# Rotary turns taken off TensorE: latent queries' last columns projected twice, local heads turned by quarters on VectorE, norm factors spread by transposes

## The chip, the cores and the metric

One core of a Trainium2 chip runs the whole program. The metric is the device time of one execution in microseconds, the median over several runs. In the rows PE is TensorE, DVE is VectorE, ACT is ScalarE, POOL is GpSimd and SP the engine whose queue issues the weight loads.

## What is computed

A first block over 512 tokens of width 1024 (spatial gating, sparse attention, cross attention to a memory, feed-forward), then two mixer layers over the 512 tokens and 256 context tokens. In each mixer layer a local branch (heads of 64) and a latent branch (heads of 64 + 32) use rotary turns. The parts that matter here:

```python
def rms_norm_2(x, g):
    xf = x.astype(jnp.float32)
    y = xf * lax.rsqrt(jnp.mean(xf * xf, axis=-1, keepdims=True) + EPS)
    return (y * g.astype(jnp.float32)).astype(x.dtype)

def apply_rope(x, cos, sin):
    xf = x.astype(jnp.float32)
    x1, x2 = jnp.split(xf, 2, axis=-1)
    c = cos[None, :, None, :]
    s = sin[None, :, None, :]
    return jnp.concatenate([x1 * c - x2 * s, x2 * c + x1 * s], axis=-1).astype(x.dtype)

def mla_project(q_lat, kv_lat, g_qa, w_qb, g_kva, w_kvb):
    B, T = q_lat.shape[:2]
    q = (rms_norm_2(q_lat, g_qa) @ w_qb).reshape(B, T, H_B, NOPE_B + ROPE_B)
...
    qa = apply_rope(qa_x.reshape(B, S, H_A, HD_A), cos_a, sin_a)
    ka = apply_rope(ka_x.reshape(B, S, HKV_A, HD_A), cos_a, sin_a)
...
    qr_x = apply_rope(qr_x, cos_b, sin_b)
```

Only the 512 tokens are turned; the context is not. H_A = 8, HKV_A = 2, H_B = 8, NOPE_B = 64, ROPE_B = 32.

## The kernel before, in words

Activations lie with features on the partitions and the tokens along the row: 768 columns (512 tokens, 256 of context), or 512 in the second layer's queries (`nt`). Each weight block arrives by DMA in one of three buffers WB; ACT copies it rounded into WH (`split_hi`), DVE takes the remainder into WL (`split_lo`), and PE multiplies high by high, high by low, low by high, so every linear is three products. `begin(name, part)` on ACT and DVE does the splits that are planned ahead at that point: before `wkvb` of half 0 it splits the query weights `wqb` of half 1; in half 1 the four first units of the next weights (`his(...)` on ACT, `los(...)` on DVE) stand there too.

Every engine's program is written by hand, and order in it is fixed. Four PSUM tiles PS0 to PS3 are given out in turn (`slot(key, *freed)`): PE waits for the marks that the last user of a tile named as `freed`. A mark is a count on a semaphore (`done`, `at`); several marks share one, as `rt`, `rc`, `qr`, `qra` share s_rope, and `qbc`, `kbc`, `qar` share s_up_a.

The latent branch, for each of two halves of four heads: PE projects the four query tiles `qb` (96 rows each, L1547 to L1562), then two key tiles `kb` with two rotations behind each (L1565 to L1580), then two value tiles `vb`, then the attention b. ACT copies a query tile from PSUM to QB (mark `qbc`). A rotation is a product of a constant matrix rotB with QB in plain f32 over 512 columns; DVE (`rope`, L2579) multiplies its result by the sines out of PSUM (`rt`), QB by the cosines (`rc`), and adds (`qr`). In program order DVE does its `begin`s, and in half 1 `los`, before the first rope. The tiles are taken anew from PS0 in each half: `qb` 0 to 3 take PS0 to PS3, `kb` 0 takes PS0, the first rotations PS1 and PS2.

The local branch: linear `kq` makes one key tile, four query tiles and one value tile (L1621); behind the first half of the next tile PE turns the tile before by the matrix rotA (`turn_tile`). ACT brings a tile to SBUF (`qar`, `kar`) before, and splits it after (`q_high`); DVE turns it (`rope_a`) and takes the low part (`q_low`). DVE's fixed order is: turn the keys, their low parts, a weight split, turn tiles 0 and 1, `q_low(0)`, `los` of four units, turn tile 2, `q_low(1)`, turn tile 3, `q_low(2)`, `q_low(3)`, and then attention a, whose softmax maxima DVE takes (L2603) before ACT can do the exponentials.

A norm's factor is one column of RS per 128 tokens; `spread_columns` (L1019) and `spread_between` (L1443) spread it over the partitions by an f32 product of the broadcast column with the identity. Marks `nrec` before and `nbc` behind. `warm` (L838) puts idle products of the identity into PE's waits.

## Time and profile before

| | us |
|---|---|
| median of 3 runs (lowest, highest) | 2468.96 (2465.03, 2470.64) |
| the profiled execution's own time | 2467.05 |
| its span in the trace | 2465.2 |
| PE busy | 2370.0 |
| DVE busy | 1545.7 |
| ACT busy | 1028.4 |
| POOL busy | 533.7 |
| mean granted TensorE clock | 0.989 of full speed |

The engines work side by side, so busy times don't add up. A stage is read from who waits for whom: in the timeline's rows the bracket gives the idle time of the engine before the instruction and what ended it. PE's records are modelled at their ends: two neighbours overlap, and the pace of PE is the distance from start to start.

### The profile page before, as it was taken

The numbers are of one execution on the slowest core, as the hardware profiler recorded it, in microseconds if no ns is written. First come the engines' busy times: TensorE is split into PE (matmuls) and PEld (weight loads), VectorE is DVE, ScalarE is ACT, GpSimd is POOL, SyncE is SP. The second block draws the span as 40 slices with busy tenths as digits, with TensorE's granted clock in tenths as the row PEclk, the third lists the DMA queues.
The fourth block names the chain that finished last, engine by engine and source line by source line (L and its number), as shares of the span: only waits on it lengthen the run. The fifth ranks groups of instructions, "written<-read, shape, count | busy, mean of one in ns | idle before, by whom it ended". The sixth has DMA issues, their size and how long they took to land.

```text
span 2465.2 us, 37427 instructions
## 1 busy us (share of the span) xinstructions
PE 2370.0 (96%) x14791; PEld 1986.9 (81%) x14791; DVE 1545.7 (63%) x2602; ACT 1028.4 (42%) x1955; POOL 533.7 (22%) x380
## 2 busy tenths in 40 slices
PE   8988999999999999999999999999999999999998
PEld 6765767777788887679977899998876688889898
DVE  4757545553434336677467867975656786788774
ACT  3337542532222235563246433334435543654343
POOL 3005212320210212231014211023623200322021
PEclk9998999999999999999999999999999999999999
DMA  5231152354532311002300122223120024013332
GB/s 193 71 104 52 36 188 69 120 160 147 168 107 88 130 50 39 27 1 69 103 26 2 43 78 60 61 78 136 50 58 29 26 69 120 10 44 114 101 110 88
DMA packets 197168, 198.72 MB, mean 81 GB/s; under 512 B 15832, under 2 KB 189624, under 8 KB 196866
## 3 DMA queue, kind: packets, MB, share of 16 engines
q1 hardware_dynamic: 191106, 178.23, 23.4%
q10 hardware_dynamic: 5888, 18.09, 2.0%
q8 instruction: 119, 1.95, 0.3%
q14 instruction: 55, 0.45, 0.1%
HBM read 186.87 MB, written 9.44 MB: 80 GB/s over the span
## 4 chain that ended last, share of the span: by engine, by line
PE 83%; DVE 9%; ACT 4%; issue 3%; POOL 1%; SPq 0%; DMA 0%; ACTq 0%; DVEq 0%; POOLq 0%
PE PS L941 9%; PE PS L942 9%; PE PS L944 9%; PE PS L895 6%; PE PS L897 6%; PE PS L896 6%; PE PS L1063 5%; PE PS L1093 4%; PE PS L868 4%; PE PS L871 4%; PE PS L869 4%; PE PS L1077 3%; DVE WL L2447 1%; PE PS L1135 1%; DVE ST L2603 1%
## 5 line engine op out<-in xcount | busy, mean ns | idle before, releaser
L2447 DVE TENSOR_TENSOR WL<-WB,WH 128x2048 fp32r<-128x2048 f32 (+3 forms) x86 | 185.8, 2160 | 208.6 <-ACT WH L1692 199.2
L941 PE MATMUL PS<-HH,WH 128*128 128x512 f32 (+4 forms) x768 | 298.1, 388 | 4.4 <-DVE XTb L3019 1.5
L942 PE MATMUL PS<-HL,WH 128*128 128x512 f32 (+4 forms) x768 | 284.9, 377 | 0.0
L944 PE MATMUL PS<-HH,WL 128*128 128x512 f32 (+4 forms) x768 | 271.4, 377 | 0.0
L3576 POOL TENSOR_SCALAR SA<-SA,ST 128x768 f32<-128x768 f32 (+4 forms) x80 | 143.7, 1796 | 512.8 <-DVE ST L2615 512.8
L1708 ACT ACTIVATE WH<-WB 128x512 fp32r<-128x512 f32 x240 | 141.9, 624 | 148.5 <-DVE WB L2459 111.8
L1692 ACT ACTIVATE WH<-WB 128x2048 fp32r<-128x2048 f32 (+3 forms) x86 | 148.0, 1721 | 131.9 <-PE PS L944 67.4
L2472 DVE TENSOR_TENSOR WL<-WB,WH 128x512 fp32r<-128x512 f32 x240 | 182.6, 775 | 32.1 <-ACT WH L1708 32.0
L895 PE MATMUL PS<-SH,WH 128*128 128x384 f32 (+1 forms) x576 | 180.6, 314 | 1.2 <-DVE WB L2506 1.2
L941 PEld LDWEIGHTS PS<-HH,WH 128*128 128x128 f32 (+2 forms) x768 | 141.6, 184 | 48.4 <-issue 8.9
L897 PE MATMUL PS<-SH,WL 128*128 128x384 f32 (+1 forms) x576 | 180.0, 313 | 0.0
L896 PE MATMUL PS<-SL,WH 128*128 128x384 f32 (+1 forms) x576 | 179.2, 311 | 0.0
L2603 DVE TENSOR_REDUCE ST<-PS 128x1 f32<-128x768 f32 (+4 forms) x176 | 129.8, 737 | 60.8 <-PE PS L1063 49.5
L942 PEld LDWEIGHTS PS<-HL,WH 128*128 128x128 f32 (+2 forms) x768 | 141.8, 185 | 30.2 <-issue 2.9
L944 PEld LDWEIGHTS PS<-HH,WL 128*128 128x128 f32 (+2 forms) x768 | 135.0, 185 | 23.6
L895 PE MATMUL PS<-HH,WH 128*128 128x384 f32 (+1 forms) x432 | 134.9, 312 | 3.6 <-DVE U L2501 2.9
L896 PE MATMUL PS<-HL,WH 128*128 128x384 f32 (+1 forms) x432 | 134.4, 311 | 0.0
L897 PE MATMUL PS<-HH,WL 128*128 128x384 f32 (+1 forms) x432 | 134.2, 311 | 0.0
L1077 PE MATMUL PS<-CM,SA 128*128 128x128 f32 x736 | 110.2, 276 | 9.0 <-ACT PTa L1805 5.0
L3551 POOL TENSOR_TENSOR RB<-RB,SA 128x512 f32<-128x512 f32 (+2 forms) x59 | 81.6, 1384 | 154.0 <-ACT SA L1758 130.7
L3724 POOL TENSOR_TENSOR YL<-SA,YH 128x768 fp32r<-128x768 f32 (+1 forms) x24 | 43.1, 1800 | 324.8 <-ACT YH L2234 324.8
L1063 PE MATMUL PS<-KB,QB 96*128 96x512 f32 (+1 forms) x288 | 105.2, 487 | 7.2 <-ACT SA L1817 7.0
(461 smaller groups left out, 6056.3 us busy)
## 6 DMA issues: line engine op xcount, KB each, us to landing
WB<-in_w_in_dram SPq DMA_DIRECT2D x61, 1024.0 KB, 5.3
WB<-in_w_ff_dram SPq DMA_DIRECT2D x32, 1024.0 KB, 5.5
WB<-in_w_mod_dram SPq DMA_DIRECT2D x24, 1024.0 KB, 5.3
WB<-in_w_branch_dram SPq DMA_DIRECT2D x24, 512.0 KB, 3.4
WB<-in_w_o_dram SPq DMA_DIRECT2D x8, 1024.0 KB, 5.4
WB<-in_w_in_dram SPq DMA_DIRECT2D x14, 512.0 KB, 6.5
WB<-in_cmp_w_dram SPq DMA_DIRECT2D x4, 1024.0 KB, 5.6
WB<-in_w_mkv_dram SPq DMA_DIRECT2D x4, 1024.0 KB, 5.1
```

The lines of the kernel that those rows point to most:

```text
L895: pe.matmul(D, wh[:, k, :], xh, start=k == 0 and not add, stop=False, skip_group_check=True)
L896: pe.matmul(D, wh[:, k, :], xl, start=False, stop=False, skip_group_check=True)
L897: t = pe.matmul(D, wl[:, k, :], xh, start=False, stop=k == 3, skip_group_check=True)
L941: pe.matmul(D[0:m, d + o:d + o + w], h, xh[:, o:o + w], start=first, stop=False)
L942: pe.matmul(D[0:m, d + o:d + o + w], h, xl[:, o:o + w], start=False, stop=False)
L944: t = pe.matmul(D[0:m, d + o:d + o + w], lo, xh[:, o:o + w], start=False, stop=last)
L1063: t = pe.matmul(S[:, o:o + n], lhs, r, start=i == 0, stop=i == len(rhs) - 1)
L1077: t = pe.transpose(T[0:w, i * 128:(i + 1) * 128], src[:, o:o + w], cm("ident"))
L1692: act.activation(b.of(WH[homes[s][0]]), b.of(WB[b.n % NW]), ACT.Copy).then_inc(*done("wh", s))
L2447: dve.tensor_tensor(b.of(WL[i]), b.of(WB[b.n % NW]), b.of(WH[i]).bitcast(F32), ALU.subtract).then_inc(*done("wl", s))
L2472: dve.tensor_tensor(place(WL, u), src, place(WH, u).bitcast(F32), ALU.subtract).then_inc(*done("wul", n))
L2603: t = dve.tensor_reduce(nm, A.S(s)[:, lo:hi], AX.X, ALU.max, negate=True)
```

## The change

Latent queries: the block `wqb` is marked `turned`. In WH and WL each head now has 128 columns: its 96, then columns 80 to 95 again, then columns 64 to 79 again. The split is three instructions on each of ACT and DVE instead of one. The projection gives 128 rows, the last 32 being the two halves of the rotary part exchanged; the sign is in the table of sines, which now has 64 rows (RPb 64 to 127). DVE multiplies rows 96 to 127 by the sines straight out of the query's PSUM tile (`turned_sines`, mark `rt`), and then the copy in QB by the cosines and adds (`add_cosines`). The sixteen rotation products of the query heads are gone, and the PSUM tile of a query now is freed by `qbc` and `rt`. The latent key's rotation stays on PE.

Local heads: rotA and `turn_tile` are gone (ten rotation products). DVE's `rope_quarters` makes the sine part with four instructions on 32 partitions each, reading one quarter and writing its neighbour, then the cosine product and the sum on 128 partitions.

Norm factors: `spread_columns`, `spread_between` and the spread of GM in front of the last linear use `pe.transpose` instead of `pe.matmul`.

```diff
+    def copies(self, W, B):
+        if not self.turned:
+            return [(self.of(W), self.of(B))]
+        w = W[:, :, :].rearrange("p a b -> p (a b)")[:, 0:self.kt * 512].rearrange("p (a b) -> p a b", b=128)
+        b = self.of(B).rearrange("p k (h c) -> p (k h) c", c=96)
+        return [(w[:, :, 0:96], b), (w[:, :, 96:112], b[:, :, 80:96]), (w[:, :, 112:128], b[:, :, 64:80])]
...
-                    t = pe.matmul(P("norm", N)[:, c * 128:(c + 1) * 128], RS[:, rs[N], c:c + 1].to_broadcast([128, 128]), cm("ident"),
-                                  start=True, stop=True)
+                    t = pe.transpose(P("norm", N)[:, c * 128:(c + 1) * 128], RS[:, rs[N], c:c + 1].to_broadcast([128, 128]), cm("ident"))
...
-                        D = slot(("qb", l, half, i), ("qbc", l, half, i))
+                        D = slot(("qb", l, half, i), ("qbc", l, half, i), ("rt", l, half, i))
...
-                        for i in (2 * p, 2 * p + 1):
-                            D = rope((half, i), ("rt", l, half, i))
-                            pe.wait_ge(*at("qbc", l, half, i))
-                            pe.matmul(D[0:96, 0:512], cm("rotB")[0:96, :], QB[0:96, i, 0:512], start=True, stop=True).then_inc(*done("rot", l, half, i))
...
-                for i, _ in enumerate(linear(f"kq{l}", hx(NT), lambda j: nt if 0 < j < 5 else NT,
-                                             lambda j: [("kar", l) if j == 0 else ("tokc", f"va{l}") if j == 5 else ("qar", l, j - 1)], pace=4)):
-                    if i % 2 and i > 1:
-                        turn_tile(i // 2 - 1)
+                drain(linear(f"kq{l}", hx(NT), lambda j: nt if 0 < j < 5 else NT,
+                             lambda j: [("kar", l) if j == 0 else ("tokc", f"va{l}") if j == 5 else ("qar", l, j - 1)]))
...
+                    def turned_sines(i):
+                        key = (l, half, i)
+                        dve.wait_ge(*at("up", "q", *key))
+                        D = taken(("rope", *key), ("qr", *key))
+                        dve.tensor_tensor(D[64:96, 0:512], P("qb", *key)[96:128, 0:512], RPb[96:128, 1, :], ALU.mult).then_inc(*done("rt", *key))
+
+                    def add_cosines(i):
+                        key = (l, half, i)
+                        x = QB[64:96, i, 0:512]
+                        dve.wait_ge(*at("qbc", *key))
+                        dve.tensor_tensor(x, x, RPb[64:96, 0, :], ALU.mult).then_inc(*done("rc", *key))
+                        dve.wait_ge(*at("rc", *key))
+                        dve.tensor_tensor(x, x, SD[sd["rope", *key]][64:96, 0:512], ALU.add).then_inc(*done("qr", *key))
                     begin(f"wqb{l}", half)
                     begin(f"wkvb{l}", half)
                     if half:
                         los(phases[run[0]][0] + 4)
-                    for p in range(2):
-                        for i in (2 * p, 2 * p + 1):
-                            rope_b((half, i), QB[0:96, i, 0:512], ("qbc", l, half, i), ("qr", l, half, i))
+                    turned_sines(0)
+                    for i in range(4):
+                        if i < 3:
+                            turned_sines(i + 1)
+                        add_cosines(i)
...
+                    for p in range(0, 128, 32):
+                        q = p + 32 if p % 64 == 0 else p - 32
+                        t = dve.tensor_tensor(D[p:p + 32, 0:512], x[q:q + 32, :], RPa[q:q + 32, 1, :], ALU.mult)
+                    t.then_inc(*done("rt", *key))
+                    dve.wait_ge(*at("rt", *key))
+                    dve.tensor_tensor(x, x, RPa[:, 0, :], ALU.mult).then_inc(*done("rc", *key))
+                    dve.wait_ge(*at("rc", *key))
+                    dve.tensor_tensor(x, x, D[:, 0:512], ALU.add).then_inc(*done(*out))
```

Where it changes the order, at three places. PE, layer 0, half 0 of the latent branch, from the last query product to the first key tile, before:

```order
L1559 MATMUL PS<-QLh,WL 96x256
L1572 MATMUL PS<-KVLh,WH 128x512 [waits s_up_v,s_up_a,s_wl]
L1573 MATMUL PS<-KVLl,WH 128x512
L1572 MATMUL PS<-KVLh,WH 128x256
L1573 MATMUL PS<-KVLl,WH 128x256
```

and now:

```order
L1566 MATMUL PS<-QLh,WL 128x256
L1579 MATMUL PS<-KVLh,WH 128x512 [waits s_rope,s_up_v,s_up_a,s_wl]
L1580 MATMUL PS<-KVLl,WH 128x512
L1579 MATMUL PS<-KVLh,WH 128x256
L1580 MATMUL PS<-KVLl,WH 128x256
```

The first product of the key tile, which writes PS0, has got a wait for s_rope; the query products have 128 rows.

DVE, layer 0, half 0: the remainder of `wkvb` (1024 columns), that of the next `wqb`, then the turns. Before:

```order
L2447 TENSOR_TENSOR WL<-WB,WH 128x1024 [waits s_wh,s_up_v]
L2447 TENSOR_TENSOR WL<-WB,WH 128x1152 [waits s_wh]
L2585 TENSOR_TENSOR SD<-PS,RPb 32x512 [waits s_hl_d,s_rpb,s_rot]
L2586 TENSOR_TENSOR QB<-QB,RPb 32x512
L2589 TENSOR_TENSOR QB<-QB,SD 32x512 [waits s_rope]
```

and now:

```order
L2445 TENSOR_TENSOR WL<-WB,WH 128x1024 [waits s_wh,s_up_v]
L2445 TENSOR_TENSOR WL<-WB,WH 128x12x96 [waits s_wh]
L2445 TENSOR_TENSOR WL<-WB,WH 128x12x16 x2
L3261 TENSOR_TENSOR SD<-PS,RPb 32x512 [waits s_hl_d,s_up] x2
L3267 TENSOR_TENSOR QB<-QB,RPb 32x512 [waits s_up_a]
L3269 TENSOR_TENSOR QB<-QB,SD 32x512 [waits s_rope]
```

The first sine product, whose mark PE now waits for, still stands behind the two splits.

DVE, layer 0, local branch: the keys' turn. Before:

```order
L2447 TENSOR_TENSOR WL<-WB,WH 128x2048 [waits s_wh]
L2585 TENSOR_TENSOR SD<-PS,RPa 128x512 [waits s_rpa,s_rope,s_rot,s_up_a]
L2586 TENSOR_TENSOR SA<-SA,RPa 128x512
L2589 TENSOR_TENSOR SA<-SA,SD 128x512 [waits s_rope]
L3397 TENSOR_TENSOR KAl<-SA,KAh 64x768 [waits s_up_a]
```

and now:

```order
L2445 TENSOR_TENSOR WL<-WB,WH 128x2048 [waits s_wh]
L3398 TENSOR_TENSOR SD<-SA,RPa 32x512 [waits s_rope,s_up_a,s_rpa]
L3398 TENSOR_TENSOR SD<-SA,RPa 32x512 x3
L3401 TENSOR_TENSOR SA<-SA,RPa 128x512 [waits s_rope]
L3403 TENSOR_TENSOR SA<-SA,SD 128x512 [waits s_rope]
L3424 TENSOR_TENSOR KAl<-SA,KAh 64x768 [waits s_up_a]
```

Six instructions stand where three stood, and none waits for PE's rotation (s_rot) any more.

## Rows read from the trace of the kernel before

**Rows 1.** The page: shares of the chain of work that ended last.

```profile
PE 83%; DVE 9%; ACT 4%; issue 3%; POOL 1%; SPq 0%; DMA 0%; ACTq 0%; DVEq 0%; POOLq 0%
```

**Rows 2.** Timeline (start us, duration us, engine line op), PE, two rotations, layer 0.

```profile
944.63 1.88 PE L1580 MATMUL PS<-QB,CM 96*96 96x512 f32 x4
945.95 0.80 PE L1572 MATMUL PS<-KVLh,WH 128*128 128x512 f32 x1
```

**Rows 3.** Sources L1580, L1612: duration ns min/median/max, first and last start.

```profile
L1580 PE MATMUL PS<-QB,CM x32: 590/592/594, 944.6 to 1921.8; 96*96 96x512 f32 x32
...
L1612 PE MATMUL PS<-SA,CM x20: 590/590/595, 1234.2 to 2099.7; 128*128 128x512 f32 x20
```

**Rows 4.** The spreads by source, and the timeline of PE at sixteen transposes.

```profile
L1024 PE MATMUL PS<-CM,RS x128: 270/275/579, 40.8 to 1836.7; 128*128 128x128 f32 x128
...
L1448 PE MATMUL PS<-CM,RS x24: 270/275/561, 1763.9 to 1802.1; 128*128 128x128 f32 x24
...
2432.88 1.91 PE L1674 MATMUL PS<-CM,XTc 128*128 128x128 f32 x16
2434.54 0.36 PE L1665 MATMUL PS<-WH,HH 128*128 128x256 f32 x1
```

**Rows 5.** Timeline, layer 0, half 0: first key tile, query weights' split, first sines.

```profile
942.55 0.39 PE L1572 MATMUL PS<-KVLh,WH 128*128 128x512 f32 x1
...
943.46 1.16 ACT L1692 ACTIVATE WH<-WB 128x1152 fp32r<-128x1152 f32 x1
...
944.64 1.36 DVE L2447 TENSOR_TENSOR WL<-WB,WH 128x1152 fp32r<-128x1152 f32 x1 [2.78 <-ACT WH L1692]
...
946.03 0.69 DVE L2585 TENSOR_TENSOR SD<-PS,RPb 32x512 f32<-32x512 f32 x1
```

**Rows 6.** Timeline, layer 0, half 1: first key tile, four units' copies, sines.

```profile
1025.02 0.39 PE L1572 MATMUL PS<-KVLh,WH 128*128 128x512 f32 x1
...
1029.11 0.69 DVE L2585 TENSOR_TENSOR SD<-PS,RPb 32x512 f32<-32x512 f32 x1
...
1031.04 0.68 DVE L2585 TENSOR_TENSOR SD<-PS,RPb 32x512 f32<-32x512 f32 x1
```

**Rows 7.** Timeline, layer 1, both halves: first key tile, DVE ahead of the sines.

```profile
1846.10 0.50 PE L1572 MATMUL PS<-KVLh,WH 128*128 128x512 f32 x1 [1.50 <-DVE WL L2447]
...
1846.32 1.62 DVE L2447 TENSOR_TENSOR WL<-WB,WH 128x1152 fp32r<-128x1152 f32 x1 [0.27 <-ACT WH L1692]
...
1914.61 0.39 PE L1572 MATMUL PS<-KVLh,WH 128*128 128x512 f32 x1
...
1918.48 0.69 DVE L2585 TENSOR_TENSOR SD<-PS,RPb 32x512 f32<-32x512 f32 x1
```

**Rows 8.** Timeline, layer 0, local branch: DVE from tile 2's turn to attention.

```profile
1263.51 0.68 DVE L2585 TENSOR_TENSOR SD<-PS,RPa 128x512 f32<-128x512 f32 x1
...
1274.04 3.91 DVE L3391 TENSOR_TENSOR QA<-SA,QA 64x768 fp32r<-64x768 f32 x4
```

**Rows 9.** Timeline, layer 1, local branch: DVE, ACT's copies, PE's start of attention.

```profile
2088.55 1.41 DVE L3391 TENSOR_TENSOR QA<-SA,QA 64x512 fp32r<-64x512 f32 x2
...
2089.59 1.28 ACT L2322 ACTIVATE QA<-SA 64x512 fp32r<-64x512 f32 x2
...
2093.98 0.68 DVE L2585 TENSOR_TENSOR SD<-PS,RPa 128x512 f32<-128x512 f32 x1
...
2102.37 2.84 DVE L3391 TENSOR_TENSOR QA<-SA,QA 64x512 fp32r<-64x512 f32 x4
...
2104.28 0.28 PE L1063 MATMUL PS<-KAh,QA 128*128 128x256 f32 x1
```

**Rows 10.** PE behind a gap; stages (start:end, length, busy, PEclk, DMA share, GB/s).

```profile
260.15 0.58 PE L941 MATMUL PS<-mnh,WH 128*128 128x256 f32 x1 [2.14 <-DVE uT L2938]
...
260.15:266.35 6.20, 6.20 (x27) 0.50 0.01 3
...
1778.90:1782.00 3.10, 3.10 (x8) 0.50 0.18 65
```

More of the change, by code:

```diff
@@ L112 @@
     flat: bool = False
+    turned: bool = False
     ring: str = ""
@@ L1447, in spread_between @@
                 for c in range(o // 128, (o + n) // 128):
-                    t = pe.matmul(P("norm", N)[:, c * 128:(c + 1) * 128], RS[:, rs[N], c:c + 1].to_broadcast([128, 128]), cm("ident"),
-                                  start=True, stop=True)
+                    t = pe.transpose(P("norm", N)[:, c * 128:(c + 1) * 128], RS[:, rs[N], c:c + 1].to_broadcast([128, 128]), cm("ident"))
                 t.then_inc(*done("nbc", N + m))
@@ L1545, in tensor_program @@
                     b = of[f"wqb{l}"][half]
-                    wh, wl = (b.of(w) for w in whole(b))
+                    wh, wl = (b.heads(w) for w in whole(b))
                     for i in range(4):
-                        D = slot(("qb", l, half, i), ("qbc", l, half, i))
+                        D = slot(("qb", l, half, i), ("qbc", l, half, i), ("rt", l, half, i))
                         if (half, i) == (0, 1):
@@ L1605, in tensor_program @@
                 merge(1)
-                def turn_tile(j):
-                    key, src = (("ka",), ("ka", l)) if j == 0 else (("qa", j - 1), ("qa", l, j - 1))
-                    D = rope(key, ("rt", l, *key))
-                    pe.wait_ge(*at(*(("qar", l, j - 1) if j else ("kar", l))))
-                    pe.matmul(D[:, 0:512], cm("rotA"), SA[sa[src]][:, 0:512], start=True, stop=True).then_inc(*done("rot", l, *key))
                 def values():
@@ L1652, in tensor_program @@
             for j in range(8):
-                t = pe.matmul(D[:, j * 128:(j + 1) * 128], GM[:, 1, 1, j, 0:1].to_broadcast([128, 128]), cm("ident"), start=True, stop=True)
+                t = pe.transpose(D[:, j * 128:(j + 1) * 128], GM[:, 1, 1, j, 0:1].to_broadcast([128, 128]), cm("ident"))
             t.then_inc(*done("tr", "gp"))
@@ L1691, in split_hi @@
                 act.wait_ge(*at(f"w{b.n % NW}", b.n))
-                act.activation(b.of(WH[homes[s][0]]), b.of(WB[b.n % NW]), ACT.Copy).then_inc(*done("wh", s))
+                for hi, w in b.copies(WH[homes[s][0]], WB[b.n % NW]):
+                    t = act.activation(hi, w, ACT.Copy)
+                t.then_inc(*done("wh", s))
             def unit_hi(n):
@@ L2446, in split_lo @@
                 i = homes[s][0]
-                dve.tensor_tensor(b.of(WL[i]), b.of(WB[b.n % NW]), b.of(WH[i]).bitcast(F32), ALU.subtract).then_inc(*done("wl", s))
+                for (lo, w), (hi, _) in zip(b.copies(WL[i], WB[b.n % NW]), b.copies(WH[i], WB[b.n % NW])):
+                    t = dve.tensor_tensor(lo, w, hi.bitcast(F32), ALU.subtract)
+                t.then_inc(*done("wl", s))
             def unit_sum(n):
```

33 lines of the change are left out of this document (17 added, 16 removed).

## The prediction

> **What bounds the kernel now.** I read the page's chain first: PE holds 83% of it [rows 1]. Then the pace of PE's starts in the stages that the change touches, and last what DVE and ACT do while PE works there. PE has almost no gaps in these stages, so an instruction taken from PE is worth its whole pace, as long as PE isn't made to wait for DVE instead. That is the question of this change: it moves the turns to DVE, and DVE's order is fixed. The profiled execution took 2467.05 us, 1.9 under the median of the runs shown; I work out a difference and add it to the median, 2468.96.
>
> **What leaves PE.** Two rotations are four passes (x4): they start at 944.63, the next product at 945.95, and it lasts 0.80 instead of the usual 0.39 [rows 2, 5]. So a pair costs 1.32 + 0.41 = 1.73 us, one rotation 0.87. There are 32 and 20 passes of them [rows 3], two to a rotation: 16 for the latent queries, 13.8 us in all, 3.46 in each of the four halves (two layers, two halves); and 10 for the local heads, 8.7 us, 4.33 in each layer. The query products get 128 rows for 96, with the same columns streamed. The key tile's products already have 128 rows, and six of them per step make a tile in 2.08 us (942.55 to 944.63, two steps [rows 2, 5]), 1.04 a step; the queries' steps of 96 rows have the same pace in the timeline. So I cost the wider products at nothing: the longer weight load lies under the product before. If it showed, by a tenth, the 12 steps of a half would take 1 us more.
>
> **The spreads.** They are 128 and 24 passes [rows 4], and 16 more of the eight products of GM: 168 for 84 products. A transpose is one pass: sixteen of them, each a record, fill 2432.88 to 2434.54, 0.104 us each [rows 4]; a pass of these spreads has nearly that pace. So 84 passes of 0.11 go: -9.3 us. They all lie on the path, since either PE is the bound or the engines behind wait for the factor. Lower bound of the gain 6 us, if those that PE does as filler inside waits (some in the cross attention) bring nothing.
>
> A row and a rule: in the attention's end the transposes of [rows 4] run among products at full pace, and nothing in the trace shows a clock that fell by them. The Trainium skill, "TensorE: Matmul & The Clock Gate", Part 4 on PE-mode transpose, says that transposes do not count as busy PE for the clock. By the row alone the spreads give 9.3; by the rule some of them, where PE is thinly busy, would let the clock fall, which is the last rival below.
>
> **Latent branch: a new wait.** The first key tile `kb` 0 takes PS0, which `qb` 0 has just left. Before, ACT's copy freed it. Now it also needs `rt` of query 0, the first sine product on DVE; and DVE does that only behind its splits, which wait for ACT, which does them behind its copy of query 3. Behind PE's waiting product stand both key tiles and both value tiles; the attention waits for those. In each half the cost is the delay of `kb` 0, less the 3.46 us of rotations.
>
> Layer 0, half 0: PE could start `kb` 0 at 942.55. ACT starts the next query weights at 943.46, 1.16 long; two short copies more (192 columns each; estimate 0.25 each, from 1.16 for 1152) end them at 945.1. DVE's remainder takes 1.36 from 944.64, now 1.3 and two short ones of 0.3 from 945.1: 946.9. The sine product, 0.69 [rows 5], ends at 947.6. PE starts 5.1 us late: net +1.6.
>
> Layer 0, half 1: DVE's `los` of four units stand ahead of the sines; the first sine product started at 1029.11 and ends at 1029.8. PE stood at `kb` 0 at 1025.02 [rows 6]: 4.8 late, net +1.3.
>
> Layer 1, half 0: PE waited already, 1.50 us up to 1846.10, for the remainder of `wkvb`. The next split ran 1846.32 to 1847.94; with ACT's and DVE's short ones it ends near 1848.9, the sines at 1849.6 [rows 7]: 3.5 later than now, net 0.
>
> Layer 1, half 1: sines end at 1919.2, PE stood there at 1914.61 [rows 7]: 4.6 late, net +1.1.
>
> The later tiles find their marks in time: DVE's three products of a turn take 1.93 us (1029.11 to 1031.04, [rows 6]), a key tile takes PE 2.08, so DVE's marks come no later than PE asks for them. Sum of the latent branch: +4.0 instead of -13.8. Bounds: -13.8 if DVE got to the sines before PE needs PS0, which these rows exclude; +8 if the short ops cost twice as much and the split's path is slower still.
>
> **Local branch.** DVE reads nothing of PE's rotation any more, but a turn has six instructions instead of three. On 32 partitions a 512-column product lasts 0.69, on 128 0.68 [rows 6, 8], and three take 1.93 together; so three more make a turn 3.87 us.
> Layer 0: the tiles of 768 columns are slow on PE, so DVE has room. Tile 2's turn started at 1263.51 [rows 8]; it follows ACT's copies, which follow PE's tile 2, earlier by three rotations: 1260.9. Then turn, `q_low(1)`, turn, the last lows: 3.87 + 1.94 + 3.87 + 3.91 = 13.6, end at 1274.5. Before it was 1274.04 + 3.91 = 1277.95 [rows 8]. The attention starts 3.5 us earlier, not 4.3.
> Layer 1: 512 columns, and PE is quick. The turn of tile 1 ended about 2088.5, before `q_low(0)` [rows 9]. Its first turn starts one rotation earlier, and two turns are 3.88 longer: 2091.5. ACT's second pair of copies, which was at 2089.59, waits for it: 1.9 later; so is what follows it, and the turn of tile 2 starts at 2093.98 + 1.9 = 2095.9. Then 3.87 + 1.41 + 3.87 + 2.84 = 12.0: 2107.9, against 2102.37 + 2.84 = 2105.2 before [rows 9]. The attention's maxima start 2.7 us later, though PE is done with the linear at 2104.28 - 4.3 = 2100.0. Sum: -0.8 instead of -8.7.
> Without anything else the change would give -9.3 + 4.0 - 0.8 = -6.1 us.
>
> **The clock.** The change makes gaps that the kernel before doesn't have: PE idle for about 5 us in each of the four latent halves (in layer 1, half 0, 1.5 of it were there), and about 5 to 7 in layer 1's local branch between the first scores and the third. The trace shows a gap of 2.14 us, and behind it the granted clock at half, 1.2 GHz instead of 2.4, from 260.15 to 266.35; in another place, behind a shorter gap, 3.10 us at half [rows 10]. Half the clock on work that PE bounds loses half of that time: 1.55 to 3.1, mean 2.3. What stands behind the latent gaps is two key and two value tiles, over 8 us of dense PE work. Five falls: +11.6 us, with 7.8 and 15.5 as bounds. A gap of 1.50 us [rows 7] is followed by products at the usual pace, so not every gap does it; but these are more than twice the one that did.
>
> **Sum.** -6.1 + 11.6 = +5.5; 2468.96 + 5.5 = 2474.5 us.
>
> **The rivals.**
> - *The clock stays up* (faster than forecast, the other side): the same waits, but no falls, or one. Then -6.1 to -4: 2463 to 2465. For it: the work before and behind the gaps is the densest of the kernel, and the 1.50 gap had none. Against: [rows 10]. It decides the sign: with fewer than three falls (6.1 / 2.3 = 2.7) the change is no loss.
> - *PE isn't made to wait at all*: the sines come early, and the whole is -9.3 - 13.8 - 8.7 = -31.8, 2437. It would need DVE ahead of ACT's copy of the query weights, against its written order and [rows 5, 6]. That the change so falls out seems nearly excluded; half of it (DVE's waits end 2 us sooner in each half) gives -14, 2455.
> - *More falls* (slower): transposes in thin places, or the wait of the local branch in layer 0 (about 2 us there before ACT's first exponentials), bring two to four falls more: +5 to +9, 2480 to 2483. For it: in the kernel as it is the clock also fell behind a gap shorter than 2.14 [rows 10], so little is wanting in thin places; the spreads of L1448 stand just before that one [rows 4, 10]. Against: only 84 products change their kind. The rule of the Trainium skill named above points to this rival.
>
> **How the numbers follow.** Forecast 0.60; clock stays up 0.17; sines early 0.08; more falls 0.15. "Same" means within 0.2%, 4.9 us, about what a measurement of this kernel can tell from no change: 2464.0 to 2473.9. The forecast's own range is 2470 to 2479 (the bounds of the clock's price); a good half of it is over 2473.9. Slower: 0.60 x 0.57 + 0.15 = 0.49. Same: 0.60 x 0.43 + 0.17 x 0.4 = 0.33. Faster: 0.17 x 0.6 + 0.08 = 0.18. For 8 in 10 the range takes in the high clock and most of the falls: 2462 to 2481.
>
> **What the profile after would show.** The first key product of each half idle 3.5 to 5.1 us behind DVE's sine product; PEclk 0.5 for 3 to 6 us right behind these; PE's third scores of layer 1's attention a idle some 7 us; the sum of the spreads' passes 84, at 0.11; six DVE ops of 0.6 to 0.7 per local turn; no L1580, no L1612. The prediction is wrong if the key tiles don't wait, if the clock stays at full behind 5 us, or if a 32-partition product is much shorter than 0.69.

## The result: 16 us slower, three times the forecast

The kernel after takes 2482.42 us (median of 5 runs, 2480.66 to 2487.06), the kernel before, beside it, 2466.76 (5 runs, 2462.70 to 2470.64). The ratio is 1.0065, with a 95% interval from 1.0050 to 1.0079: 12 to 20 us more. The forecast was +5.5 us, 2474.5, with 2481 as the upper end of its range: the sign was right, the size was not, and the time is 1.4 us outside the range.

The page of the kernel after: busy times, and the shares of the chain that ended last.

```profile
PE 2353.1 (95%) x14655; PEld 1983.2 (80%) x14655; DVE 1569.3 (63%) x2640; ACT 1031.0 (42%) x1963; POOL 535.2 (22%) x380
...
PE 80%; DVE 10%; ACT 4%; issue 3%; POOL 1%; SPq 0%; DMA 0%; ACTq 0%; DVEq 0%; POOLq 0%
```

The sources of its spreads (duration ns min/median/max, first and last start):

```profile
L1033 PE MATMUL PS<-CM,RS x64: 270/273/475, 40.7 to 1838.4; 128*128 128x128 f32 x64
...
L1456 PE MATMUL PS<-CM,RS x12: 270/272/454, 1769.5 to 1804.7; 128*128 128x128 f32 x12
```

PE's share of the chain went from 83% [rows 1] to 80%, DVE's from 9% to 10%: PE has less to do and waits more. The spreads are 64 and 12 passes where there were 128 and 24 [rows 4]; there are no rotations of queries and local heads left [rows 3].

Where the time goes is read by laying the two traces on each other. The table takes the start of the same ACT instruction in both profiled executions (spans 2465.2 and 2480.6).

| point | before | after | after - before | in the stage |
|---|---|---|---|---|
| layer 0: first latent query copied | 930.68 | 926.27 | -4.4 | -4.4 |
| half 1: first latent query copied | 1015.84 | 1015.55 | -0.3 | +4.1 |
| local branch: key tile's heads copied | 1240.20 | 1242.66 | +2.5 | +2.8 |
| first local output copied | 1287.90 | 1292.47 | +4.6 | +2.1 |
| layer 1: first latent query copied | 1835.71 | 1838.01 | +2.3 | -2.3 |
| half 1: first latent query copied | 1908.58 | 1912.89 | +4.3 | +2.0 |
| local branch: key tile's heads copied | 2076.75 | 2083.73 | +7.0 | +2.7 |
| first local output copied | 2114.74 | 2130.54 | +15.8 | +8.8 |
| end | 2465.2 | 2480.6 | +15.4 | -0.4 |

The spreads gain where they stand alone, in the first stage and at the change of layers (how far the first stage differs between executions comes below). Each latent half loses 2.0 to 4.1 us. The largest loss is a single stage: the local branch of layer 1.

The first latent half of after, on three engines (timeline: start us, duration us, engine, line, operation, idle time before it and what ended that; then a stage: length, busy us of PE, its weight loads, DVE, ACT and POOL, granted clock, DMA share, GB/s). First the timeline, then the stage:

```profile
938.36 1.65 ACT L1688 ACTIVATE WH<-WB 128x1152 fp32r<-128x1152 f32 x3
...
940.05 1.90 DVE L2445 TENSOR_TENSOR WL<-WB,WH 128x1152 fp32r<-128x1152 f32 x3 [3.27 <-ACT WH L1688]
941.97 1.31 DVE L3261 TENSOR_TENSOR SD<-PS,RPb 32x512 f32<-32x512 f32 x2
...
942.93 0.76 PE L1579 MATMUL PS<-KVLh,WH 128*128 128x512 f32 x1 [5.31 <-DVE SD L3261]
```

```profile
943.00:949.00 6.00, 6.00 (x19) 5.12 (x20) 5.74 (x10) 1.61 (x2) 0.00 (x0) 0.50 0.60 177
```

This is what answers to [rows 5]: PE stands 5.31 us ahead of its first key product, since the sine product of query 0 comes behind DVE's share of a split (L2445), and that behind ACT's copies of the same weights. Those weights are the *next* query block's, which nobody needs yet. Behind the wait PE runs at a granted clock of 0.50, here for the whole 6 us. The other three halves have the same pair of a wait (4.76, 5.10, 4.55 us) and a stretch at 0.50; with the trace cut into slices of 1 us, each of the four stretches is 6.8 us long.

Layer 1's local branch of after (timeline, as above, and one stage):

```profile
2104.69 2.77 DVE L3398 TENSOR_TENSOR SD<-SA,RPa 32x512 f32<-32x512 f32 x4
2107.50 0.69 DVE L3401 TENSOR_TENSOR SA<-SA,RPa 128x512 f32<-128x512 f32 x1
2108.23 0.69 DVE L3403 TENSOR_TENSOR SA<-SA,SD 128x512 f32<-128x512 f32 x1
2108.95 1.40 DVE L3418 TENSOR_TENSOR QA<-SA,QA 64x512 fp32r<-64x512 f32 x2
...
2115.95 0.81 ACT L1781 ACTIVATE SA<-PS 128x768 f32<-128x768 f32 x1
...
2116.82 0.58 PE L1071 MATMUL PS<-KAh,QA 128*128 128x256 f32 x1 [8.31 <-ACT SA L1781]
2123.60 0.69 PE L1071 MATMUL PS<-KAh,QA 128*128 128x384 f32 x1 [2.60 <-ACT VA L2352]
...
2117.71 0.69 DVE L2602 TENSOR_REDUCE ST<-PS 128x1 f32<-128x513 f32 x1
```

```profile
2114.00:2126.00 12.00, 6.59 (x28) 5.76 (x29) 7.71 (x15) 5.22 (x10) 1.58 (x1) 0.50 0.00 0
```

A turn takes from 2104.69 to 2108.95, 4.26 us; the first maxima of the attention start at 2117.71; PE waits 8.31 us for ACT's copy of the values' tile and then 2.60 us more, for another copy of ACT (L2352), ahead of the fourth scores; and the clock is at 0.50 for the whole 12 us. The wait of 8.31 us stands ahead of the second scores, whose PSUM tile the linear's last tile, the values', still holds. Layer 0 has the same waits, the first one shorter (timeline of PE, after):

```profile
1277.45 0.39 PE L1071 MATMUL PS<-KAh,QA 128*128 128x256 f32 x1 [1.76 <-ACT SA L1781]
...
1280.60 0.69 PE L1071 MATMUL PS<-KAh,QA 128*128 128x384 f32 x1 [1.68 <-ACT SA L1814]
...
1284.87 0.69 PE L1071 MATMUL PS<-KAh,QA 128*128 128x384 f32 x1 [2.60 <-ACT VA L2352]
```

There the clock is at 0.50 from about 1280.2 for 10.2 us: it fell in the wait of 1.68 us, ahead of the one of 2.60. In layer 1 it is at 0.50 for 13.7 us. In the kernel before, PE waits 0.64 and 0.70 us for the same copy (L2355), one step later, and the clock stays up in both local branches.

### The profile page after: what moved, and what is told of

Same layout as the page of the kernel before. It is cut to its first block, busy times and chain, and to the rows that moved or that the text cites. A ratio compares the mean times of both kernels' runs of the same rounds, so it can differ in the third digit from the quotient of the medians.

```text
span 2480.6 us, 37187 instructions
## 1 busy us (share of the span) xinstructions
PE 2353.1 (95%) x14655; PEld 1983.2 (80%) x14655; DVE 1569.3 (63%) x2640; ACT 1031.0 (42%) x1963; POOL 535.2 (22%) x380
## 3 DMA queue, kind: packets, MB, share of 16 engines
q8 instruction: 118, 1.93, 0.3%
## 4 chain that ended last, share of the span: by engine, by line
PE 80%; DVE 10%; ACT 4%; issue 3%; POOL 1%; SPq 0%; DMA 0%; ACTq 0%; DVEq 0%; POOLq 0%
PE PS L950 9%; PE PS L951 8%; PE PS L953 8%; PE PS L904 6%; PE PS L906 6%; PE PS L905 6%; PE PS L1071 5%; PE PS L1101 4%; PE PS L877 4%; PE PS L880 4%; PE PS L878 4%; PE PS L1085 3%; DVE WL L2445 1%; DVE WL L2471 1%; PE PS L1143 1%
## 5 line engine op out<-in xcount | busy, mean ns | idle before, releaser
L2445 DVE TENSOR_TENSOR WL<-WB,WH 128x2048 fp32r<-128x2048 f32 (+4 forms) x94 | 186.1, 1986 | 211.1 <-ACT WH L1688 201.2
L953 PE MATMUL PS<-HH,WL 128*128 128x512 f32 (+4 forms) x768 | 270.4, 376 | 0.0
L1688 ACT ACTIVATE WH<-WB 128x2048 fp32r<-128x2048 f32 (+4 forms) x94 | 150.1, 1605 | 133.0 <-PE PS L953 67.5
L953 PEld LDWEIGHTS PS<-HH,WL 128*128 128x128 f32 (+2 forms) x768 | 134.4, 184 | 24.3
```

The source lines that it names most:

```text
L953: t = pe.matmul(D[0:m, d + o:d + o + w], lo, xh[:, o:o + w], start=False, stop=last)
L1688: t = act.activation(hi, w, ACT.Copy)
L2445: t = dve.tensor_tensor(lo, w, hi.bitcast(F32), ALU.subtract)
```

## The experiments

The question was where the 10 us beyond the forecast come from. Theories: (1) the latent halves: more or longer falls of the clock than the forecast's five; (2) the local branch: slower turns, the new wait of 2.60 us and what hangs on it; (3) the spreads by transposes let the clock fall. Ratios are against the kernel before, on the same chip, and are turned into us with 2467 us.

### The three parts, each alone

The kernel before with one part of the diff applied. Of the spreads, at three places:

```
-                    t = pe.matmul(P("norm", N)[:, c * 128:(c + 1) * 128], RS[:, rs[N], c:c + 1].to_broadcast([128, 128]), cm("ident"),
-                                  start=True, stop=True)
+                    t = pe.transpose(P("norm", N)[:, c * 128:(c + 1) * 128], RS[:, rs[N], c:c + 1].to_broadcast([128, 128]), cm("ident"))
```

Of the latent part (with `copies`, `heads` and the products on all 128 rows, as in the change):

```
-                            D = rope((half, i), ("rt", l, half, i))
-                            pe.matmul(D[0:96, 0:512], cm("rotB")[0:96, :], QB[0:96, i, 0:512], start=True, stop=True).then_inc(*done("rot", l, half, i))
...
+                            turned_sines(i + 1)
+                        add_cosines(i)
```

Of the local part:

```
-                        turn_tile(i // 2 - 1)
...
+                    rope_quarters((l, "qa", j), D, ("qar", l, j), ("qra", l, j))
```

> The kernel before with one part of the change alone: the norms' factors are spread over the partitions by transposes, not by products. Theory A (the trace of after beside that of before: at the same instruction ahead of the first latent half after is 5.1 us early, at the layer change it gains another 3.4): this part alone gives about -9 us against before (2456 to 2460), with the clock's rows of before elsewhere. Theory B (the rival of the prediction in which transposes don't hold the clock up): the clock falls in the thin places where the spreads stand and the run comes out between -5 and +3 us.

> The kernel before with the latent part of the change alone (last columns of the latent queries projected twice, no rotation for them on TensorE). Theory A (drift of after against before over the four latent halves: +4.8, +3.6, +2.8, +3.5 us): about +14.7 us against before, a wait of 4.5 to 5.3 us ahead of the keys of each half, and 6 to 7 us at clock 0.5 behind each. Theory B (the misses of the halves come from what the other parts did to the clock or the queues): about +4 us, as the waits alone would give, with fewer than four falls of the clock.

> The kernel before with the local part of the change alone (local heads turned by quarters on VectorE). Theory A (drift of after against before over the local branches: +1.7 in layer 0, +7.5 in layer 1): about +9 us against before, with a turn of 4.26 us, waits of 2.6 us ahead of the fourth scores of both layers, a wait of some 8 us ahead of the second scores of layer 1, and the clock at 0.5 for some 10 us in either branch. Theory B (the local branch of after is late only because of what the spreads and the latent part left in the queues): -0.8 us, the forecast of the prediction for this part, give or take 3.

| part alone | ratio (95%) | us | forecast for it |
|---|---|---|---|
| spreads | 0.9970 (0.9959 to 0.9981) | -7.4 | -9.3 |
| latent | 1.0053 (1.0040 to 1.0066) | +13.1 | +4.0, and four falls of 2.3: +13.2 |
| local | 1.0037 (1.0023 to 1.0050) | +9.1 | -0.8, and one fall: +1.5 |

They add up to +14.8, against +16.0 for all together: the intervals show no action of the parts on one another. The latent branch came out as forecast; the forecast for the spreads lies in their interval; the local branch is 7.6 us off, the largest part of the miss of 10.5 (of the rest, 1.9 lies in the spreads and 1.2 between this sum and the whole).

The spreads alone, a chain of six passes in the first query tile of layer 0, and before, twelve (timeline):

```profile
927.37 0.81 PE L1024 MATMUL PS<-CM,RS 128*128 128x128 f32 x6
928.02 1.50 PE L841 MATMUL PS<-CM 128*128 128x128 f32 x12
```

```profile
930.49 1.50 PE L1024 MATMUL PS<-CM,RS 128*128 128x128 f32 x12
931.82 0.94 PE L841 MATMUL PS<-CM 128*128 128x128 f32 x7
```

Six passes in 0.65 us against twelve in 1.33: 0.11 us a pass, as costed. Theory 3 falls as the cause of the 10 us, since this part alone is 7.4 us faster, near its forecast. In the thin place where the spreads of L1448 stand, the granted clock of the kernel with this part alone is a little higher, not lower (kernel with the spreads alone, then before; the stages differ a little in length):

```profile
1756.00:1804.00 48.00, 43.56 (x235) 36.94 (x235) 38.92 (x68) 18.49 (x32) 22.67 (x21) 0.89 0.23 70
```

```profile
1760.00:1804.00 44.00, 40.88 (x219) 35.35 (x218) 32.47 (x55) 14.80 (x25) 20.00 (x18) 0.84 0.25 77
```

A small effect on the clock is neither shown nor excluded. Over the whole span, in slices of 1 us, this kernel is at half the clock for 63.6 us and before for 54.8, and it has one stretch that before has not: 3.4 us from 1278, in layer 0's local branch. But such stretches also come and go between executions of the same code.

### The latent halves: wait and clock apart

Earlier turning steps on DVE, in front of its shares of the next splits:

```
-                    begin(f"wkvb{l}", half)
-                    if half:
-                        los(phases[run[0]][0] + 4)
                     turned_sines(0)
                     for i in range(4):
                         if i < 3:
                             turned_sines(i + 1)
                         add_cosines(i)
+                    begin(f"wkvb{l}", half)
+                    if half:
+                        los(phases[run[0]][0] + 4)
```

> After, with VectorE's eight turning steps of a latent half placed ahead of its shares of the splits of the next weights, instead of behind them; same instructions otherwise. Theory A (the waits ahead of the keys of each half come from the queue of VectorE, which stands behind a split that waits for ScalarE's copies, and the clock falls because of these waits): the four waits of 4.6 to 5.3 us go below 1.5 us, the clock stays at 1.0 in these stretches, and the run is 20 to 27 us shorter than after (about 2455 to 2462). Theory B (the waits are those of the sines' own length, or the split is needed by the keys): the waits stay over 3 us and the run is at most 8 us shorter (2474 or more).

Ratio 0.9951 (0.9939 to 0.9963), median 2455.49: 28 us below after and 12 below before, by one change of order. Three of the four waits are gone. In layer 1, half 0, PE still waits 2.47 us for the sine product (before waited 1.50 there), which is over the 1.5 that theory A allowed. The clock stays up in all four halves (timeline, and the first half's stage behind where its wait had been):

```profile
938.28 1.31 DVE L3261 TENSOR_TENSOR SD<-PS,RPb 32x512 f32<-32x512 f32 x2
...
939.23 0.47 PE L1579 MATMUL PS<-KVLh,WH 128*128 128x512 f32 x1
...
946.69 1.63 DVE L2445 TENSOR_TENSOR WL<-WB,WH 128x1152 fp32r<-128x1152 f32 x2
...
1833.52 0.47 PE L1579 MATMUL PS<-KVLh,WH 128*128 128x512 f32 x1 [2.47 <-DVE SD L3261]
```

```profile
938.00:944.00 6.00, 5.86 (x36) 4.96 (x35) 5.74 (x10) 4.28 (x7) 0.00 (x0) 1.00 0.58 178
```

The split (L2445) now starts over 6 us later than in after (946.69, not 940.05), and no wait of PE for it is seen. The gain is 1 us over the upper end of what theory A expected.

The clock by itself: PE kept busy in the wait.

```
+                    pe.wait_ge(*at("qbc", l, half, 0))
+                    warm(PS[0], 20)
                     for p in range(2):
                         D = slot(("kb", l, half, p), ("kbc", l, half, 2 * p + 1))
```

> After, with 20 products of the identity by itself on TensorE (0.21 us each at 2.4 GHz, results not used) in the wait ahead of the keys of each latent half, to hold its clock up; the waits themselves stay. Theory A (the fall of the clock behind each wait is a cost of its own, 6 to 7 us at half rate, some 3 us lost each time): no stretch at 0.5 there, 9 to 13 us shorter than after (2469 to 2474). Theory B (what follows the wait is bound by VectorE or ScalarE, not by TensorE's clock): the clock stays up and the run is within 3 us of after (2479 to 2485).

Ratio 1.0031 (1.0019 to 1.0042), 2474.01 us: 8.4 us below after by the ratios, a little less than theory A expected. PE does 4.62 us of idle products, in 40 passes, and goes on 0.70 us later at full clock (timeline and stage):

```profile
936.06 4.62 PE L850 MATMUL PS<-CM 128*128 128x128 f32 x40
941.38 0.47 PE L1581 MATMUL PS<-KVLh,WH 128*128 128x512 f32 x1 [0.70 <-issue]
```

```profile
941.00:947.00 6.00, 5.62 (x36) 5.10 (x37) 5.74 (x10) 2.71 (x4) 0.00 (x0) 1.00 0.59 175
```

The keys come no sooner than in after relative to their queries (in layer 1, half 0, 0.9 us later), and still 8.4 us are back: 2.1 us for each of the four falls, against 2.3 in the forecast. The intervals leave 4 to 5 us either way on the 8.4, and the traces show why it varies. From the first key product to the first product of the attention, PE takes 8.4 to 8.5 us in the kernel with the early turning steps; in after it takes 10.7 to 11.3, and in a second profiled execution of after (below) 9.8 to 10.1, with only 3.4 us at half the clock in each half. A fall so costs 2.3 to 2.8 us in the one and 1.3 to 1.6 in the other. In the latent branch the clock costs about 8 us, then, and the remainder of the 28, some 20, goes with the waits themselves: PE's idle time ahead of the keys fell from 19.7 us in all to 2.5.

The Trainium skill, "TensorE: Matmul & The Clock Gate", Part 1, says that the low clock is the default and that activity of the array releases it. This run agrees: products whose results nobody reads held the clock at 1.00 in all four halves.

### The local branch: a tile that moved

With the rotations gone, the ring of PSUM tiles in `kq` is taken six times, not eleven. So the values' transposes get the third of the four tiles, where they had the fourth. The attention on PE waits for these tiles at fixed steps, `first_use = {..., 3: [2], 4: [3]}` (L1099 of before): the third is asked for one step earlier, before the fourth scores, and ACT frees it (its copy L2352) only behind its third exponential. The edit gives the tile its old place:

```
                 def values():
                     yield
+                    ps.order = [3, 0, 1, 2]
                     to_tok(f"va{l}", 128, NT, ("va", l))
```

> After, with the tile of PSUM that takes the local values' transposes in the place that it had before (the fourth, not the third), in both layers; no other edit. Theory A (the wait of 2.60 us ahead of the fourth scores of either local branch, for ScalarE's copy of the values, comes from this tile's place): both waits go and the run is 3 to 5 us shorter than after (2477 to 2480). Theory B (the first softmax steps are bound by VectorE's maxima there, and the copy is waited for one step later): under 1.5 us shorter, with a like wait ahead of the fifth scores.

Median 2473.17 us, ratio 1.0032 (1.0020 to 1.0043), some 8 us below after, more than either theory expected. But its profiled execution took 2483.29 us, the longest of its nine, and it was 4.1 us behind after's ahead of the first latent half, in a part where both kernels have the same instructions. So it was run once more, beside after again:

> The kernel after once more, unchanged, to tell how far its profiled execution and its times repeat. Theory A (the time is a property of the program): 2479 to 2485 us, with the same waits of 5.31, 4.76, 5.10 and 4.55 us ahead of the keys and 8.31 and 2.60 us in the second local branch. Theory B (the first look was a high one): about 2473 us, as the median of the kernel with the values' tile in its old place, whose profiled execution took 2483.

> The kernel after with the values' tile of PSUM in its place of before, once more. Its first profiled execution was 4.1 us later than after already ahead of the first latent half, where the two programs are the same, and gained 3.3 us over the local branches. Theory A (the tile is worth what the two waits of 2.60 us are, less what comes due next): 3 to 4 us below after on the same chip. Theory B (it is worth the 9 us between the medians): 8 to 10 us below.

After came to 2482.35 us, ratio 1.0067 (1.0054 to 1.0080): it repeats. The kernel with the tile came to 2476.12, ratio 1.0043 (1.0029 to 1.0056): 5.9 us below after on the same chip, between the two theories. The first latent copy of the same code started at 926.27 and 926.29 us in after's two profiled executions, at 930.34 and 928.74 in this kernel's; so a few us come and go ahead of these stages, and the stages are compared from a mark inside them. The traces show where they come from: at one and the same product of the cross attention (the one of [rows 10] behind the gap of 2.14 us) this kernel's first profiled execution is at 264.45 and after's at 260.37, 4.1 us apart already, while near 178 they were together; in between the clock is at half for 27.3 us in a row in the one and for 17.1 in the other. From the key tile's copy on ACT to the first exponential, and from there to the first output (before, after, and after with the tile; layer 1, timeline of ACT):

```profile
2076.75 3.41 ACT L2337 ACTIVATE KAh<-SA 64x768 fp32r<-64x768 f32 x4
...
2106.22 0.69 ACT L1817 ACTIVATE SA<-PS,ST 128x513 f32<-128x513 f32 x1 [0.87 <-DVE ST L2603]
...
2114.74 0.27 ACT L1825 ACTIVATE Y<-PS 128x128 f32<-128x128 f32 x1
```

```profile
2083.73 3.42 ACT L2334 ACTIVATE KAh<-SA 64x768 fp32r<-64x768 f32 x4
...
2118.50 0.69 ACT L1814 ACTIVATE SA<-PS,ST 128x513 f32<-128x513 f32 x1 [1.74 <-DVE ST L2602]
...
2130.54 0.29 ACT L1822 ACTIVATE Y<-PS 128x128 f32<-128x128 f32 x1
```

```profile
2080.13 3.41 ACT L2335 ACTIVATE KAh<-SA 64x768 fp32r<-64x768 f32 x4
...
2114.91 0.69 ACT L1815 ACTIVATE SA<-PS,ST 128x513 f32<-128x513 f32 x1 [1.74 <-DVE ST L2603]
...
2124.25 0.28 ACT L1823 ACTIVATE Y<-PS 128x128 f32<-128x128 f32 x1
```

| us | layer 0: key to exp | exp to output | layer 1: key to exp | exp to output |
|---|---|---|---|---|
| before | 38.76 | 8.94 | 29.47 | 8.52 |
| local part alone | 37.11 | 12.22 | 34.77 | 11.72 |
| after | 37.11 | 12.70 | 34.77 | 12.04 |
| after, tile in its old place | 37.11 | 9.79 | 34.78 | 9.34 |

The first column of each layer repeats to 0.02 us in every kernel with quarters in which the order of DVE and ACT in this branch is that of after: it is DVE's queue. The second is the tile: 2.9 and 2.7 us, 5.6 in all. (In the other profiled executions the second column is 12.24 and 12.71 for after, 9.98 and 8.95 with the tile.) Both waits of 2.60 us are gone; of the wait for this copy 0.33 us is left in layer 1, at 2120.01. The clock still falls in both branches, but for a shorter time: 6.8 and 10.2 us at half, against 10.2 and 13.7 in after (10.2 and 17.1 in its second profiled execution). So the fall in layer 0 doesn't come from the tile; it came with the quarters (the local part alone has it too), with which PE waits ahead of the second and third scores. No run filled these waits with idle products, so the clock's own share in the local branches is not measured.

### Is it ACT's order or DVE's queue that holds layer 1?

```
                 q_high(2)
+                to_tok(f"va{l}", 5, 128, NT)
                 q_high(3)
-                to_tok(f"va{l}", 5, 128, NT)
```

> After, with ScalarE's copy of the local values placed ahead of its copy of the last query tile's heads, not behind it. Theory A (in layer 1 the first softmax waits for VectorE, whose four turns and splits end 12 us later than before; the wait of 8.31 us on TensorE for the values' copy only shows it): that wait goes or shrinks by more than 3 us, the first maxima of layer 1 stay at about 2117.7 us, and the run is less than 3 us shorter. Theory B (the copy's place in ScalarE's queue is what holds the branch): 6 to 8 us shorter (2474 to 2476).

Ratio 1.0058 (1.0046 to 1.0071), 2480.93 us: 1 to 2 us below after, less than the intervals can tell from nothing. PE's gaps in layer 1 (timeline), and DVE's first maxima:

```profile
2109.18 0.39 PE L1071 MATMUL PS<-KAh,QA 128*128 128x256 f32 x1 [2.64 <-ACT SA L1781]
2117.38 0.69 PE L1071 MATMUL PS<-KAh,QA 128*128 128x384 f32 x1 [6.59 <-ACT SA L1814]
...
2115.77 0.69 DVE L2602 TENSOR_REDUCE ST<-PS 128x1 f32<-128x513 f32 x1
```

The wait of 8.31 us became one of 2.64 and, one step on, one of 6.59 that wasn't there. The first maxima start 33.99 us after the key tile's copy (2081.78), in after 33.98 (2083.73 to 2117.71). So the wait that the trace shows on PE is not the cause: DVE's queue is, with its turns, its splits and the low parts of the queries. The last run below confirms it from the other side: with the shares of the splits taken out (2.5 us on DVE, 2.2 on ACT) the first maxima come 3.3 and 3.1 us sooner behind the key tile's copy. It is on this queue that a turn of 4.26 us, not 3.87, costs time.

### Versions that beat both kernels

First both edits together on the kernel after, the early turning steps and the tile's old place:

> Both edits on the kernel after: VectorE's turning steps of the latent halves ahead of its splits, and the values' tile of PSUM in its place of before. Theory A (they act at different places and add): 3 to 9 us below the first edit alone (2446 to 2452), the local rotations off TensorE still. Theory B (the tile's gain in the first run came from the clock and doesn't repeat): within 2 us of 2455.5.

Ratio 0.9931 (0.9918 to 0.9943), 2448.36 us, as theory A expected. The two edits add: 28 and 5.6 us one by one, 34 found together against after. It is 7.1 us below the first edit alone by the medians, on another chip.

The local heads' rotations given back to TensorE (`turn_tile`, `rotA` and the order of before), the early turning steps and the spreads kept:

```
-                    rope_quarters((l, "qa", j), D, ("qar", l, j), ("qra", l, j))
+                    rope((l, "qa", j), [(D, 0, 128)], D, ("qar", l, j), RPa[:, 0, :], RPa[:, 1, :], ("qra", l, j), 0, ("rpa", l))
...
+                        turn_tile(i // 2 - 1)
```

> After, with the local heads' rotation back on TensorE as before, and VectorE's turning steps of the latent halves ahead of the splits: spreads and latent part of the change in the order that costs no wait. Theory A (spreads -8 to -9, latent part -13.8 from TensorE if nothing waits and the clock stays): 2443 to 2448, below both kernels. Theory B (the halves are held by VectorE or ScalarE whatever the order): about 2456 to 2463, no better than the spreads alone.

Ratio 0.9922 (0.9910 to 0.9934), 2446.55 us, as theory A expected, the lowest median here, 19 us below before. It and the one above can't be told apart: their intervals overlap. With the tile in place and the halves in order, these runs show no difference between turning the local heads on TensorE and by quarters. Its layer 1 has 29.48 us from the key's copy to the first exponential, as before, where the quarters have 34.76; that the PE time which the quarters save pays for this is the likely reason and was not measured by itself.

One edit more, on the kernel with both edits: the share of the next weights' splits moved ahead of the key's turn, into DVE's idle time there (5.25 us in layer 1 of after).

```
                 begin(f"kq{l}")
+                his(phases[run[0]][0] + 4)
...
                 begin(f"kq{l}", 2)
-                his(phases[run[0]][0] + 4)
                 q_in(3)
```

(and `los` on DVE likewise.)

> The kernel with both edits (turning steps of the latent halves ahead of the splits, values' tile of PSUM in its old place), and in the local branches the share of the next weights' splits on ScalarE and VectorE (2.2 and 2.5 us) placed ahead of the key's turn, in VectorE's idle 5 us there, not between the second and third query's turns. Theory A (the queue of VectorE from the key's turn to the last query's low parts is what the first softmax of layer 1 waits for, and nearly that of layer 0): the first maxima come 2 to 2.5 us earlier in each layer, and the run is 3 to 5 us below the two edits alone (2443 to 2446). Theory B (the splits in front make the key's turn late, since their weights are not there or ScalarE's copies hold the key's tile back): no shorter, 2448 to 2451.

Ratio 1.0073 (1.0055 to 1.0092), 2485.09 us: 35 us above the kernel that it started from (37 by the medians, on another chip). Theory A was right on the queue: from the key tile's copy to the first maxima it takes 33.05 and 30.90 us, where it took 36.32 and 33.98. But the key tile itself comes 23 us later in layer 0, which is theory B, at a price that neither theory had. In layer 0 (timeline):

```profile
1241.86 2.19 ACT L1706 ACTIVATE WH<-WB 128x512 fp32r<-128x512 f32 x4 [30.93 <-PE PS L953]
...
1242.53 2.50 DVE L2472 TENSOR_TENSOR WL<-WB,WH 128x512 fp32r<-128x512 f32 x4 [29.26 <-ACT WH L1706]
...
1257.37 0.76 PE L950 MATMUL PS<-HH,WH 128*128 128x512 f32 x1 [15.55 <-DVE WL L2446]
```

ACT's copies write into places of `WH` that PE's `kq` products (L953) still read: ACT waited 30.93 us for them with the key's tile behind it in its queue, DVE 29.26 for ACT, and PE 15.55 for DVE. DVE's idle time was free; the place that the split writes to was not.

## Why the forecast was wrong, step by step

- **Spreads, -9.3:** right in mechanism, and in size within the interval. 84 passes went, at 0.11 us; alone they measure -7.4 (-10.1 to -4.7). The rival *more falls*, as far as it goes by transposes, doesn't explain the miss. The Trainium skill, "TensorE: Matmul & The Clock Gate", Part 4, says that transposes don't count as busy for the clock in the same way. No run here shows an effect of that clearly. Ahead of the first latent half, the eleven traces with transposes have 37.5 to 54.5 us at half the clock, the three without 34.1 to 37.5; that leaves room for an effect of up to 3 us (an estimate: among the eleven, each us more at half goes with some 0.3 us more up to that half, and the means differ by 8 us).
- **Latent branch, a new wait, +4.0:** right in mechanism. The waits were forecast to make PE 5.1, 4.8, 3.5 and 4.6 us late; in the trace it stands idle 5.31, 4.76, 5.10 and 4.55 us, the third with 1.50 that was there [rows 7], so 3.60 more. Wait and queue were the ones named: the sines behind a split behind ACT. The part alone measures +13.1 against 13.2 with the falls.
- **Clock, 2.3 us a fall:** right for the latent halves (8.4 us for four by the run with idle products), with some luck: 2.3 is the mean of two stretches of other places, 6.20 and 3.10 us [rows 10], and the stretches here are 6.8 us in one profiled execution and 3.4 in another. Five falls were forecast, four there and one in the local branch of layer 1; there were six, the sixth in layer 0's local branch, which only the rival *more falls* had, with the wait that it named. Those two last longer than costed: 10.2 and 13.7 us at 0.50 instead of at most 6.2. The forecast's idle time of some 7 us in layer 1 was placed ahead of the third scores; it is 8.31 us and stands ahead of the second.
- **Local branch, -0.8:** this is the step that failed, by 7.6 us together with its fall (+1.5 forecast, +9.1 measured). Three things are in it. *First*, the turn was costed at 3.87 us, from three overlapping instructions of 1.93 in all, doubled; it takes 4.26, since the four products of the quarters don't overlap. Two turns are on the chain in layer 0 and four in layer 1, up to 0.8 and 1.6 us. In the run of this part alone the first exponentials start at 1277.53 and 2114.21 (before: 1278.96 and 2106.22), where it was already 1.1 and 3.5 us late at the latent copies ahead of them (931.78 and 1912.12): 2.5 us early in layer 0 (forecast 3.5) and 4.5 late in layer 1 (forecast 2.7), 2.8 us of the miss. *Second*, the place of the values' tile in PSUM. From the first exponential to the first output this run takes 3.3 and 3.2 us more than before, where the forecast had 2.3 for one fall: 4.2 of the miss. With the tile put back on the kernel after, 5.6 us go. The prediction followed the ring of PSUM tiles in the latent branch, where it found the new wait, and not in the local one, where five takes less shift the tile; nothing in its sum or its rivals stands for it. *Third*, the clock there, which can't be split from the second, since the tile in its old place also shortens the stretches at 0.50 (from 10.2 and 13.7 us to 6.8 and 10.2).
- **The rivals.** *The clock stays up* fell: all four halves fell to 0.50. *PE isn't made to wait at all* was given 0.08 for the kernel as written, and rightly; put in order, its mechanism is worth 28 us. That it would need DVE ahead of ACT's copies was the point, and it cost one moved block. *More falls* had 2480 to 2483 us, and the time lies in it; but it came to that by two to four falls more and had nothing for the turn and the tile. One fall more was there, so the number is mostly luck.
- **The range.** It took in two to four falls more as its upper case and nothing for a part that is simply mis-sized. The two terms with the least trace behind them, the local branch's chain and the clock, were given bounds one by one and not together: with 2481 as the end it had 6.5 us above the forecast, and the local branch alone missed by 7.6.

What stays open: whether the 1.2 us between the sum of the parts (+14.8) and the whole (+16.0) are real, which the intervals can't tell; what the falls in the local branches cost apart from the waits; and why the clock is at half for 17.1 us in one execution and for 27.3 in another, in code that is the same.

## What to carry to other kernels

When instructions that take a buffer are removed, every later take of that ring moves: follow the ring to the next fixed wait, not only the time that the instructions took. When work is moved to an engine with a written order, put it ahead of whatever there waits for a third engine and isn't needed soon; here that order was worth 28 us. But a split may be moved forward only as far as the place that it writes to is free.

## What the hardware showed that was not expected

A product of DVE on 32 partitions takes as long as one on 128 (0.69 and 0.68 us for 512 columns), and four in a row, each on other partitions than the one before, don't overlap as other ones do. Four quarters take 2.77 us, 0.69 each. In before the first product of a turn starts at 2093.98 [rows 9] and its second 0.61 later (timeline of DVE, before):

```profile
2094.59 0.68 DVE L2586 TENSOR_TENSOR SA<-SA,RPa 128x512 f32<-128x512 f32 x1
```

The Trainium skill, "VectorE: DVE Perf Modes", section "Two Vector instructions with no wait between them", says that an instruction whose input or output starts in another group of 32 partitions than that of the one before starts only when all earlier ones have finished. The quarters change their group each time, and their pace of 0.69 agrees; so do the two sine products of the latent heads above, which stay in their groups and take 1.31 us together, 0.63 from start to start.

In the local branches of after the clock stays at half for 10.2 to 17.1 us, in its latent halves, where dense products follow the wait, for 3.4 to 6.8. Idle products of PE in the wait bring back 2.1 us a fall, and in three of the four halves the keys are not later for it. And the time at half differs between executions of the same code, by 10 us in one place of the cross attention.
